# Order of VectorE's maximum, scaling and gating in the latent attention rounds of a two-block model kernel

## What is computed

```python
def mla_attend(q_nope, q_rope, k_nope, k_rope, v):
    s = (jnp.einsum('bqhd,bkhd->bhqk', q_nope, k_nope) + jnp.einsum('bqhr,bkr->bhqk', q_rope, k_rope)) * MLA_SCALE
    p = jax.nn.softmax(s, axis=-1).astype(v.dtype)
    return jnp.einsum('bhqk,bkhd->bqhd', p, v)

o_ml = mla_latent_blocks(qn_l, qr_l, concatenate([kn_c, kn_l]), concatenate([krot_c, krot_l]), concatenate([vm_c, vm_l]))
y_mla = o_ml * jax.nn.silu(mg_l)
y_lat = jnp.einsum('bne,ed->bnd', jnp.concatenate([y_gla, y_mla], -1), w_out)
```

## Time and profile before

| | us |
|---|---|
| median of 3 runs | 1402.22 |
| the profiled execution, its own time | 1402.47 |
| its span in the trace | 1401.1 |
| TensorE matmul busy in the span | 1094.1 (78%) |
| VectorE busy | 477.2 (34%) |
| ScalarE busy | 332.3 (24%) |
| the latent rounds, first scores to last pair's product | 1224.0 to 1282.5 |

### The profile page before, as it was taken

The page is one execution under the profiler, slowest core; times in us unless marked ns, Lnnn a source line. Parts: engine busy times, 40 slices in busy tenths (PEclk is TensorE's granted clock), DMA queues, the critical chain, the costliest instruction groups (busy, mean ns, idle before and its releaser), DMA issues.

```text
span 1401.1 us, 19376 instructions
## 1 busy us (share of the span) xinstructions
PE 1094.1 (78%) x8447; PEld 618.9 (44%) x8447; DVE 477.2 (34%) x978; ACT 332.3 (24%) x639; POOL 96.7 (7%) x135
## 2 busy tenths in 40 slices
PE   8999776697576557999996656766555699999998
PEld 7666211353231112897641211212111189754897
DVE  6577122001211000878620100100000078665775
ACT  4543100010410000474210000000000056443640
POOL 2221100000000000050121000000000000010100
PEclk9999878899688867999997877778887899999999
DMA  9969999999999999958999999999999994423720
GB/s 349 401 254 396 421 428 428 428 426 428 427 428 428 427 427 422 384 202 340 372 416 425 427 427 428 428 427 427 428 428 428 421 387 151 181 76 137 294 122 31
DMA packets 45829, 501.04 MB, mean 358 GB/s; under 512 B 9478, under 2 KB 10772, under 8 KB 16304
## 3 DMA queue, kind: packets, MB, share of 16 engines
q1 hardware_dynamic: 40408, 491.93, 84.2%
q10 hardware_dynamic: 2696, 6.57, 1.3%
q0 software_dynamic: 2640, 1.29, 0.3%
HBM read 498.67 MB, written 1.10 MB: 357 GB/s over the span
## 4 chain that ended last, share of the span: by engine, by line
PE 47%; DMA 46%; DVE 3%; ACT 2%; issue 1%; SPq 1%; POOL 0%; ACTq 0%; DVEq 0%; POOLq 0%
DMA weight_ring<-in_moe_w_gate_up 32%; DMA weight_ring<-in_u_down 8%; PE bank L1623 7%; PE bank L383 4%; PE bank L384 4%; PE bank L385 4%; PE bank L382 4%; PE bank L1657 3%; DMA weight_ring<-in_u_ctx_kv 2%; DMA weight_ring<-in_u_last 2%; PE bank L2090 2%; PE bank L675 2%; PE bank L2302 1%; PE bank L428 1%; PE bank L1086 1%; PE bank L1253 1%
## 5 line engine op out<-in xcount | busy, mean ns | idle before, releaser
L1623 PE MATMUL bank<-weight_ring,expert_tokens 128*32 128x512 f32 x1840 | 276.3, 735 | 148.4 <-DMA weight_ring<-in_moe_w_gate_up 144.1
L1623 PEld LDWEIGHTS bank<-weight_ring,expert_tokens 128*32 128x32 f32 x1840 | 58.9, 122 | 334.8 <-DMA weight_ring<-in_moe_w_gate_up 187.9
L1657 PE MATMUL bank<-weight_ring,actT 128*32 128x256 f32 x1920 | 155.2, 482 | 60.5 <-DMA weight_ring<-in_u_down 50.6
L1867 DVE TENSOR_TENSOR act<-silu,bank 128x256 f32<-128x256 f32 x32 | 13.4, 420 | 379.3 <-ACT silu L1994 379.3
L1657 PEld LDWEIGHTS bank<-weight_ring,actT 128*32 128x32 f32 x1920 | 71.4, 133 | 133.5 <-DMA weight_ring<-in_u_down 55.3
L1994 ACT ACTIVATE silu<-bank 128x256 f32<-128x256 f32 x32 | 12.3, 384 | 432.8 <-PE bank L1623 432.8
L1882 DVE COPY expert_outs<-bank 32x256 f32<-32x256 f32 x60 | 25.1, 418 | 228.7 <-PE bank L1657 227.7
L423 DVE TENSOR_TENSOR weight_ring_rounded<-weight_ring,weight_ring_rounded 128x1024 fp32r<-128x1024 f32 (+1 forms) x84 | 98.5, 1231 | 10.2 <-ACT weight_ring_rounded L407 10.0
L407 ACT CAST weight_ring_rounded<-weight_ring 128x1024 fp32r<-128x1024 f32 (+1 forms) x80 | 77.8, 1046 | 15.4 <-DMA weight_ring<-in_u_qkv 7.0
L2013 ACT COPY expert_outs<-bank 32x256 f32<-32x256 f32 x60 | 21.9, 364 | 199.6 <-PE bank L1657 198.8
L557 POOL TENSOR_TENSOR norm_rstd<-norm_var,minus_half 128x1 f32<-128x1 f32 x12 | 11.7, 974 | 809.3 <-DVE norm_var L1917 631.0
(11 more groups left out here) (558 smaller groups left out, 1865.4 us busy)
## 6 DMA issues: line engine op xcount, KB each, us to landing
weight_ring<-in_moe_w_gate_up SPq DMA_DIRECT2D x115, 2048.0 KB, 36.1
weight_ring<-in_u_down SPq DMA_DIRECT2D x60, 2048.0 KB, 37.1
weight_spare<-in_moe_w_gate_up SPq DMA_DIRECT2D x11, 2048.0 KB, 40.3
weight_ring<-in_u_ada SPq DMA_DIRECT2D x8, 2048.0 KB, 8.9
weight_ring<-in_u_last SPq DMA_DIRECT2D x16, 512.0 KB, 33.4
weight_ring<-in_u_lru SPq DMA_DIRECT2D x4, 2048.0 KB, 25.2
weight_spare<-in_u_ada SPq DMA_DIRECT2D x3, 2048.0 KB, 13.5
weight_ring<-in_u_qkv SPq DMA_DIRECT2D x2, 2048.0 KB, 16.0
```

Of the source, the lines that this page charges most:

```text
L1623: last = pe.matmul(up[CAP * j:CAP * (j + 1), :], self.expert_tokens(t, e), w[:, :, j, :], start=(t == 0), stop=(t == T - 1))
L1657: last = pe.matmul(K[3][CAP * q:CAP * (q + 1), 0:QC], B.actT[i][:, s, j * CAP:(j + 1) * CAP], w[:, jj, s, q, :], start=(j == 0 and s == 0) ...
```

## The change

VectorE's pass is put in another order: first the wait for scores n, their maximum and its scaling, then the reciprocal and the scaling of the probabilities n - 2. The gating of the head pairs goes from passes 7, 11, 15, 19 to passes 8, 12, 16, 20, and the loop has one pass more. TensorE's and ScalarE's programs are not edited.

```diff
-        for n in range(NB + 4):
+        for n in range(NB + 5):
+            if n < NB:
+                v.wait_ge(*sig.after("scores_lat", n))
+                v.tensor_reduce(B.lat_neg[:, n:n + 1], self.latent_bank("s", n), AX.X, ALU.max).then_inc(*sig.tell("latent_steps"))
+                v.wait_ge(*sig.now("latent_steps"))
+                v.tensor_scalar(B.lat_neg[:, n:n + 1], B.lat_neg[:, n:n + 1], -MSCALE, None, ALU.mult).then_inc(
+                    *sig.tell("latent_steps", ("neg_lat", n)))
             if 2 <= n < NB + 2:
                 i = n - 2
                 v.wait_ge(*sig.after("exp_lat", i))
                 v.reciprocal(B.lat_tot[:, i:i + 1], B.lat_tot[:, i:i + 1]).then_inc(*sig.tell("latent_steps"))
                 v.wait_ge(*sig.now("latent_steps"))
                 v.tensor_scalar(B.pr[i % 3], B.pr[i % 3], B.lat_tot[:, i:i + 1], None, ALU.mult).then_inc(
                     *sig.tell("latent_steps", ("probs_lat", i)))
-            if n < NB:
-                v.wait_ge(*sig.after("scores_lat", n))
-                v.tensor_reduce(B.lat_neg[:, n:n + 1], self.latent_bank("s", n), AX.X, ALU.max).then_inc(*sig.tell("latent_steps"))
-                v.wait_ge(*sig.now("latent_steps"))
-                v.tensor_scalar(B.lat_neg[:, n:n + 1], B.lat_neg[:, n:n + 1], -MSCALE, None, ALU.mult).then_inc(
-                    *sig.tell("latent_steps", ("neg_lat", n)))
             if n in (2, 4):
                 kt = n - 1
                 v.wait_ge(*sig.after("latent", MH + kt))
                 v.tensor_copy(B.vals_lat[:, kt, :], K[7]).then_inc(*sig.tell("vector_moved", ("latent_taken", MH + kt)))
-            if n >= 7 and n % 4 == 3:
-                j = n // 4 - 1
+            if n >= 8 and n % 4 == 0:
+                j = n // 4 - 2
                 v.wait_ge(*sig.after("values_lat", j))
```

## The result

The changed kernel takes 1428.63 us (median of 5 runs, 1425.23 to 1429.97) against 1402.22 us before (5 runs, 1400.03 to 1403.51): a ratio of 1.0185, 95% interval 1.0173 to 1.0198, some 26 us slower. The profiled execution has a span of 1428.5 us.

What follows compares the result with a forecast made beforehand. TensorE was taken as the bound; stalls of 20.2 us in rounds 5 to 15, plus 2.8 for rounds 2 to 4, less 2.7 of replaced idle time, gave 20.3 us more: 1422.5 us, range 1417 to 1429.

Steps and rivals of the forecast that it cites:

- The bound: Latent rounds: TensorE sets the pace, scores followed at once by transposes; only in rounds 7 to 10 it idles, 2.67 us.
- The price of a stalled round: Rounds 5 to 15: transposes n-2 wait behind scores n and their maximum, 1.84 us a round, 20.2 us in all.
- 22 to 23 us of waits in the profile: Sign: some 14 waits of TensorE's transposes for the wide scaling in rounds 2 to 15, against 2.4 us before.
- Rounds 2 to 4: The values product partly covers the stall: 0.98 us each in rounds 2 and 3, 0.8 in round 4, together 2.8.
- What the new stall replaces: Rounds 8 and 10: TensorE's existing idle time is replaced by the new stall, not added to it: minus 2.7 us.
- Part 2: Head pairs gated a round later, with two rounds of slack left: nothing, plus or minus 0.4 us.
- Absorption: From 1292 us on the rest of the kernel moves as a block; none of the 20 us is taken back.
- The clock: Rival: same stalls, and TensorE's clock falls one to four times between rounds 5 and 15, 1424 to 1429 us; chance 0.30.
- clock kept: Main case: stall of 1.84 us in 11 rounds with the clock held, 1419 to 1426 us; chance 0.57.
- The price of one fall: A fall of TensorE's clock to 1.2 GHz costs 3.42 - 1.92 = 1.5 us, from 16 matmuls.
- The other side: Rival: earlier maximum frees VectorE in rounds 7 to 10, TensorE's 2.67 us idle goes, 1399.5 us; chance 0.02.

Runs made afterwards that it cites:

- five rounds alone: The kernel before, with the maximum ahead of the scaling in rounds 11 to 15 only, gating as before: 1411.22 us, ratio 1.0067.
- filled kernel: The changed kernel with 7 unused 128x128 identity products between TensorE's scores and its wait for probabilities in rounds 5 to 15: 1423.41 us, ratio 1.0150.
- kernel with rounds 5 to 10 alone: The kernel before, with the maximum ahead of the scaling in rounds 5 to 10 only, gating as before: 1419.76 us, ratio 1.0129.
- last experiment: Kernel before with late gating, transposes a round later, and linear branch's transposes, gating and output products a pass later: 1402.29 us, ratio 0.9996.

## Why the prediction was right, and where it was not

- **The bound.** Right. TensorE sets the pace and the chain runs through scores and transposes. Both kernels that keep the maximum out of that chain (late gating alone, transposes a round later) are at 1402 to 1403 us.
- **The price of a stalled round.** Right: 2.67 us from scores to transposes forecast, 2.68 measured, so a stall of 1.82 us for 1.84; in five rounds alone, 9.2 forecast and 9.18 measured. The forecast of 22 to 23 us of waits in the profile was too high, 20.7 came: it took the stalls from start to start, and 0.16 us of each does not show as idle time.
- **Rounds 2 to 4.** Right: 2.78 us forecast for round 2 and 2.79 measured; its wait is 0.80 us, that of round 4 0.87.
- **What the new stall replaces.** Mis-sized by 0.5 us. I took the idle time of the busy view, 2.67 us. From start to start the old waits cost more: scores to transposes 1249.49 - 1247.16 = 2.33 us in round 8 and 1254.74 - 1252.58 = 2.16 in round 10, each less 0.86, and the second linear transposes (L2772) came 1250.79 - 1249.96 = 0.83 us after the first instead of 0.44. That is 1.47 + 1.30 + 0.39 = 3.16 us. With it the sum is 19.8 us; the filled kernel's stage shows 19.1.
- **Part 2, nothing within 0.4 us.** Right: the stage with it alone differs by 0.05 us, and the interval of its ratio holds 1.
- **Absorption.** Right: none; 114.8 us from the residual to the end in both.
- **The clock.** This is the step that failed. I held "clock kept" for the likeliest (0.57) and the fall for a rival (0.30); the fall happened, in each of the kernels that stalled through rounds 5 to 10 and had nothing to fill the stalls. The time of 1428.63 us is that of the rival, 1424 to 1429 us, and 6 us above the single number. The reason I gave against it, that 1015:1029 kept its clock at 8.20 of 14 us busy, came from a stretch cut off too early. The next rows of the same trace of before are

```profile
1028.43 2.48 PE L1623 MATMUL bank<-weight_ring,expert_tokens 128*32 128x512 f32 x16 [2.98 <-DMA weight_ring<-in_moe_w_gate_up]
...
1029.00:1030.00 1.00, 1.00 (x16) 0.14 (x6) 0.00 (x0) 0.00 (x0) 0.00 (x0) 0.83 1.00 426
```

so the clock fell within a microsecond of the end of that stretch. The price of one fall was too low too: 1.5 us, from 16 matmuls. There the fall lasted for one group of matmuls. Here three falls held for 10, 7 and 7 us, and cost 9.4 us together in the profiled execution, 3.1 us each. That the measured median lies in the stated range, 1417 to 1429 us, is in part luck: it is 0.4 us from the edge, two of the five runs lie beyond it, and the edge stands on up to four falls of 1.5 us, where there were three of 3.1.
- **The other side.** TensorE had no work between scores and transposes, as the forecast said, so an earlier maximum brought it nothing. Of the 2.67 us of idle time that this rival wanted back, the last experiment's stage shows 1.5 us gained.

## What to carry to other kernels

Before two steps are swapped in one engine's queue, ask of each what the other engines do between the event that it waits for and the result that stands behind it; if there is nothing, the whole distance is a stall in every round, and the bound engine pays it. Price TensorE's stalls twice, once as time and once as clock, and look for places where little work stands between two of them. A stall that can't be taken out is cheaper when filled, provided the filling is measured to fit.

## What was not expected of the hardware

- Stalls of 1.66 us in the records, none longer, took the clock to 1.2 GHz three times, in rounds 5 to 10. A run of them was not needed for the first fall: it came within the first such stall in the changed kernel, and behind a single one in the kernel with rounds 5 to 10 alone. The same stalls in rounds 11 to 15 kept 1.00, in the changed kernel and in the one with those rounds alone. From the transposes to the end of the next scores TensorE has, by the timeline of the kernel before, 1.5 to 3.5 us of work in rounds 5 to 10, and by that of the changed kernel 3.2 to 5.3 us in rounds 11 to 15. The two overlap, so the runs show where the clock fell and not what exactly it takes. The fall of the rows ahead of the prediction came after 2.98 us of idle time. The Trainium skill (TensorE: Matmul & The Clock Gate, "What's actually happening") has the gate set by how busy the engine has been recently. The runs agree as far as they go: the clock fell only in kernels with empty stalls in rounds 5 to 10, and held at 1.00 in the two where these were filled.
- A 128x128 float32 product of the identity has two records and takes 0.22 us (2.90 / 13), not the 0.11 us of one transposes record.
- Filling raised TensorE's busy time from 1102.1 us in the changed kernel's page to 1116.7 us, and the time fell by 5.2 us.
